# Second mixer to its feed-forward: squares from PSUM, x renewed in pairs of tiles, squares of x in the mixer, summed by TensorE in two halves

## What is computed

```
u_glu, q, k, v, gate_logits = split((rms_norm(x, pre_norm1) * (1 + sc1) + sh1) @ w_in)
...
y = (g_conv * y_conv + g_att * y_att) @ w_o
x = x + g1 * rms_norm(y, post_norm1)
h = rms_norm(x, pre_norm2) * (1 + sc2) + sh2
f = square(relu(h @ w_ff1)) @ w_ff2
x = x + g2 * rms_norm(f, post_norm2)
```

## Time and profile before

| | us |
|---|---|
| median of 3 runs (2768.16 to 2770.42) | 2768.65 |
| the profiled execution, its own time | 2776.59 |
| the profiled execution, span in the trace | 2774.8 |
| TensorE busy | 2628.9 (95%) |
| VectorE busy | 1464.5 (53%) |
| ScalarE busy | 926.0 (33%) |
| GpSimd busy | 1120.2 (40%) |
| granted TensorE clock, mean | 0.965 |

### The profile page before, as it was taken

The page is one execution under the profiler, slowest core; times in us unless marked ns, Lnnn a source line. Parts: engine busy times, 40 slices in busy tenths (PEclk is TensorE's granted clock), DMA queues, the critical chain, the costliest instruction groups (busy, mean ns, idle before and its releaser), DMA issues. The chain is left out here.

```text
span 2774.8 us, 32389 instructions
## 1 busy us (share of the span) xinstructions
PE 2628.9 (95%) x12740; PEld 2086.6 (75%) x12740; DVE 1464.5 (53%) x1794; ACT 926.0 (33%) x1314; POOL 1120.2 (40%) x505
## 2 busy tenths in 40 slices
PE   6999999999999999999999999599999999699997
PEld 4777778788888777778788887487776677488886
DVE  7884434843334885435753333498635563533333
ACT  4332443322223433343322221343234533222222
POOL 3333334344443433334344443178922223244442
PEclk9999999999999999999999999799989989799998
DMA  5222222343334222222343342232211112122331
GB/s 158 69 69 81 73 79 92 115 143 121 121 106 146 79 67 80 69 77 91 99 147 126 126 129 79 89 91 78 89 54 46 46 38 91 54 91 92 98 98 53
DMA packets 226619, 253.40 MB, mean 91 GB/s; under 512 B 9024, under 2 KB 202944, under 8 KB 226240
## 3 DMA queue, kind: packets, MB, share of 16 engines
q1 hardware_dynamic: 226176, 251.18, 28.8%
q10 hardware_dynamic: 320, 0.52, 0.1%
HBM read 246.96 MB, written 4.19 MB: 91 GB/s over the span
## 5 line engine op out<-in xcount | busy, mean ns | idle before, releaser
L217 POOL TENSOR_TENSOR sb_w_lo<-sb_raw,sb_w_hi 128x1024 fp32r<-128x1024 f32 x404 | 983.6, 2446 | 1416.7 <-ACT sb_w_hi L212 1414.9
L239 PE MATMUL ps<-sb_a_hi,sb_w_hi 128*128 128x512 f32 x1472 | 607.9, 413 | 35.6 <-POOL sb_w_lo L217 18.2
L212 ACT ACTIVATE sb_w_hi<-sb_raw 128x1024 fp32r<-128x1024 f32 x404 | 422.7, 1056 | 616.5 <-PE ps L241 537.8
L240 PE MATMUL ps<-sb_a_lo,sb_w_hi 128*128 128x512 f32 x1472 | 590.5, 401 | 0.0
L241 PE MATMUL ps<-sb_a_hi,sb_w_lo 128*128 128x512 f32 x1472 | 589.9, 401 | 0.0
L239 PE MATMUL ps<-sb_b_hi,sb_w_hi 128*128 128x512 f32 x960 | 381.3, 397 | 7.9 <-PEq L189 4.3
L239 PEld LDWEIGHTS ps<-sb_a_hi,sb_w_hi 128*128 128x128 f32 x1472 | 282.3, 192 | 134.6 <-issue 31.1
L240 PE MATMUL ps<-sb_b_lo,sb_w_hi 128*128 128x512 f32 x960 | 380.2, 396 | 0.0
L241 PE MATMUL ps<-sb_b_hi,sb_w_lo 128*128 128x512 f32 x960 | 380.0, 396 | 0.0
L241 PEld LDWEIGHTS ps<-sb_a_hi,sb_w_lo 128*128 128x128 f32 x1472 | 281.6, 191 | 69.5
L240 PEld LDWEIGHTS ps<-sb_a_lo,sb_w_hi 128*128 128x128 f32 x1472 | 282.6, 192 | 65.6 <-issue 2.4
(11 more groups left out here) (342 smaller groups left out, 2878.3 us busy)
## 6 DMA issues: line engine op xcount, KB each, us to landing
sb_raw<-in_w_in_dram SPq DMA_DIRECT2D x148, 512.0 KB, 3.7
sb_raw<-in_w_ffn_in_dram SPq DMA_DIRECT2D x88, 512.0 KB, 4.9
sb_raw<-in_w_ff_dram SPq DMA_DIRECT2D x64, 512.0 KB, 3.8
sb_ada<-in_w_ada_dram SPq DMA_DIRECT2D x48, 512.0 KB, 4.5
sb_raw<-in_w_ffn_out_dram SPq DMA_DIRECT2D x44, 512.0 KB, 3.8
sb_raw<-in_w_mix_o_dram SPq DMA_DIRECT2D x16, 512.0 KB, 3.4
sb_raw<-in_w_conv_o_dram SPq DMA_DIRECT2D x8, 512.0 KB, 3.4
sb_raw<-in_w_attn_o_dram SPq DMA_DIRECT2D x8, 512.0 KB, 3.3
```

The lines of the kernel that those rows point to most:

```text
L212: act.activation(w_hi[:, s, :], raw[:, s, :], ACT.Copy).then_inc(hi_done[s], 1)
L217: pool.tensor_tensor(w_lo[:, s, :], raw[:, s, :], w_hi[:, s, :].bitcast(F32), ALU.subtract)\
L239: pe.matmul(out, wh, hi, start=first and i == 0, stop=False)
L240: pe.matmul(out, wh, lo, start=False, stop=False)
```

## The change

In the mixer's "wo" groups ScalarE squares both tiles straight from PSUM, and then scales them by `gain_post` into `att` as it copies them; the banks come free after that. VectorE adds tiles 1 to 6 only, and TensorE sums tiles 0 and 7 with `n_sq=2`. VectorE and GpSimd renew x in pairs of tiles, in the form of the end of `ffn2`. ScalarE squares the renewed x into `c_pair_32` while still in the mixer, in the order of pairs 1, 0, 3, 2. The gains of `ffn2` are formed in the mixer, into columns 32 to 48 of `mod`, and the load of `par` in `ffn2` is gone. In `ffn2` TensorE begins with the sums over tiles 0 to 3 and over tiles 4 to 7, 16 matmuls each, and VectorE puts the two together with two small operations; ScalarE's squares and VectorE's adds are gone there. The counts of the semaphores shift accordingly.

```diff
@@ -142,6 +142,7 @@
         mod = mod_t[:, :]
+        ffn_gains = mod_t[:, 32:48]
         ps = top.enter_context(nc.psum_tensor("ps", [P, 8, T], F32))
@@ -1692,14 +1693,11 @@
                 act_in = sb(st, "f2_act_in", [P, 2, T])
-                par = sb(st, "f2_par", [P, NP2_COLS])
-                scale = sb(st, "f2_scale", [P, 16])
+                scale = ffn_gains
...
                     def _(sp):
-                        sp.dma_start(par[:, :], d["par2"][:, 0:NP2_COLS]).then_inc(small_in, 16)
-
@@ -1758,7 +1756,13 @@
                     def _(pe):
-                        pe_norm(pe, sq)
+                        pe_sum(pe, sq[:, 0:4, :], SUM_BANK, n_sq=4)
+                        for n in range(NB):
+                            for kt in range(4, KD):
+                                ins = pe.matmul(ps[:, SUM_BANK, NB + n:NB + n + 1], sq[:, kt, n * P:(n + 1) * P], ones[:, 0:1],
+                                                start=kt == 4, stop=kt == KD - 1)
+                        ins.then_inc(sums_done, 1)
+                        pe_spread(pe, rstd, SPREAD_BANK, rstd_done, 0)
                         h = [(h_hi[:, i, :], h_lo[:, i, :]) for i in range(KD)]
@@ -1813,14 +1817,13 @@
                         down(last_u + ups + 3, 0, last % 2, bank=0, start=False, tile_done=down_tile)
-                        pe.wait_ge(square_sum, 2)
-                        pe.wait_ge(squares, 2 * KD)
+                        pe.wait_ge(square_sum, 1)
+                        pe.wait_ge(squares, KD)
                         pe_sum(pe, sq[:, 0:KD:KD - 1, :], SUM_BANK, n_sq=2)
...
                     def _(act):
-                        act_squares(act, x, sq)
                         for n in range(rounded, SLOTS):
@@ -1868,16 +1871,13 @@
                         tt, ts, stt = dve.tensor_tensor, dve.tensor_scalar, dve.scalar_tensor_tensor
-                        dve.wait_ge(small_in, 16)
                         gain = scale[:, 0:8]
-                        step.done(stt(gain, mod[:, 32:40], 1.0, par[:, P2["pre_norm2"][0]:P2["pre_norm2"][1]],
-                                      ALU.add, ALU.mult))
-                        step.done(tt(scale[:, 8:16], mod[:, 40:48], par[:, P2["post_norm2"][0]:P2["post_norm2"][1]],
-                                     ALU.mult))
                         cm = Count(dve, mean_done)
                         nd = Count(dve, normed)
-                        dve_add_squares(dve, step, sq)
-                        dve_mean(dve, SUM_BANK, 0, cm)
+                        dve.wait_ge(sums_done, 2)
+                        half = rstd[:, NB:2 * NB]
+                        step.done(ts(half, ps[:, SUM_BANK, 0:NB], 1.0 / D, EPS, ALU.mult, ALU.add))
+                        cm.done(stt(rstd[:, 0:NB], ps[:, SUM_BANK, NB:2 * NB], 1.0 / D, half, ALU.mult, ALU.add))
                         dve.wait_ge(spread, 1)
@@ -1919,8 +1919,8 @@
                         def add_square(kt):
-                            dve.wait_ge(squares, KD + kt + 1)
-                            (Count(dve, square_sum, 1) if kt == KD - 2 else step).done(
+                            dve.wait_ge(squares, kt + 1)
+                            (Count(dve, square_sum) if kt == KD - 2 else step).done(
                                 tt(sq[:, 0, :], sq[:, 0, :], sq[:, kt, :], ALU.add))
@@ -1934,7 +1934,7 @@
                                 add_square(kt - 1)
-                        dve_mean(dve, SUM_BANK, 1, cm)
+                        dve_mean(dve, SUM_BANK, 2, cm)
                         dve.wait_ge(spread, 2)
@@ -2120,9 +2120,11 @@
                         pool_rsqrt(pool, 3)
-                        for kt in range(1, KD, 2):
-                            pool.wait_ge(x_done, 3 * (kt // 2) + 3)
-                            pool.tensor_tensor(x[:, kt, :], x[:, kt, :], q[:, kt, :], ALU.add).then_inc(x_done_odd, 1)
+                        pool.wait_ge(x_back, 16)
+                        for p in range(0, 4, 2):
+                            pool.wait_ge(pair_scaled, p // 2 + 1)
+                            two = slice(2 * p, 2 * p + 2)
+                            pool.tensor_tensor(x[:, two, :], x[:, two, :], q[:, two, :], ALU.add).then_inc(x_done_odd, 1)
@@ -2240,7 +2242,8 @@
-                        pe_sum(pe, conv, SUM_BANK, square_sum, 2)
+                        pe.wait_ge(squares, 3 * KD + KD)
+                        pe_sum(pe, conv[:, 0:KD:KD - 1, :], SUM_BANK, square_sum, 2, n_sq=2)
                         pe_spread(pe, rstd, SPREAD_BANK, rstd_done, 3)
@@ -2366,10 +2369,16 @@
-                                act.activation(att[:, two, :], src, ACT.Copy).then_inc(done, 1)
-                                emptied(act, gi)
-                                for t in (2 * p, 2 * p + 1):
-                                    act.activation(conv[:, t, :], att[:, t, :], ACT.Square).then_inc(squares, 1)
+                                for o in range(2):
+                                    act.activation(conv[:, 2 * p + o, :], src[:, o, :], ACT.Square).then_inc(squares, 1)
+                                for o in range(2):
+                                    t = 2 * p + o
+                                    ins = act.activation(att[:, t, :], src[:, o, :], ACT.Identity, scale=gain_post[:, t:t + 1],
+                                                         bias=0.0)
+                                    if o:
+                                        ins.then_inc(done, 1)
+                                    else:
+                                        step.done(ins)
                             if 17 <= gi <= 20:
@@ -2388,6 +2397,14 @@
+
+                        for p in (1, 0, 3, 2):
+                            if p % 2:
+                                act.wait_ge(x_done, p // 2 + 1)
+                            else:
+                                act.wait_ge(x_done_odd, p // 2 + 1)
+                            for t in (2 * p, 2 * p + 1):
+                                act.activation(c_pair_32[:, t, :], x[:, t, :], ACT.Square).then_inc(squares, 1)
@@ -2416,6 +2433,8 @@
                         step.done(tt(gain_post, mod[:, 16:24], pcol("post_norm1", 0, 8), ALU.mult))
+                        step.done(stt(ffn_gains[:, 0:8], mod[:, 32:40], 1.0, pcol("pre_norm2", 0, 8), ALU.add, ALU.mult))
+                        step.done(tt(ffn_gains[:, 8:16], mod[:, 40:48], pcol("post_norm2", 0, 8), ALU.mult))
                         step.done(ts(head_gain, pcol("head_norm"), 1.0 - LAM_INIT, None, ALU.mult))
@@ -2569,16 +2588,24 @@
                                 prod_rest(HEADS2 - 1, gc[:, HEADS2 - 1, :])
-                        dve_add_squares(dve, step, conv, 3 * KD, 1)
+                        for kt in range(1, KD - 1):
+                            dve.wait_ge(squares, 3 * KD + kt + 1)
+                            (Count(dve, square_sum, 1) if kt == KD - 2 else step).done(
+                                tt(conv[:, 0, :], conv[:, 0, :], conv[:, kt, :], ALU.add))
+                        dve.wait_ge(squares, 3 * KD + KD)
                         dve_mean(dve, SUM_BANK, 4, cm)
...
                         dve.wait_ge(x_back, 16)
-                        xd = Count(dve, x_done)
-                        for kt in range(KD):
-                            xd.done(stt(x[:, kt, :], x[:, kt, :], gain_post[:, kt:kt + 1], ps[:, SPREAD_BANK, :],
-                                        ALU.mult, ALU.mult))
-                            if kt % 2 == 0:
-                                xd.done(tt(x[:, kt, :], x[:, kt, :], q[:, kt, :], ALU.add))
+                        emptied(dve, len(G2) - 2)
+                        emptied(dve, len(G2) - 1)
+                        scaled_pair, xd = Count(dve, pair_scaled), Count(dve, x_done)
+                        row = ps[:, SPREAD_BANK, :].unsqueeze(1).to_broadcast([P, 2, T])
+                        for p in range(0, 4, 2):
+                            first, other = slice(2 * p, 2 * p + 2), slice(2 * p + 2, 2 * p + 4)
+                            scaled_pair.done(tt(x[:, first, :], x[:, first, :], row, ALU.mult))
+                            there = ps[:, p:p + 2, :]
+                            step.done(tt(there, x[:, other, :], row, ALU.mult))
+                            xd.done(tt(x[:, other, :], there, q[:, other, :], ALU.add))
                 phase_end()
```

## The result

The changed kernel is slower. Against the kernel before on the same chip the ratio is 1.0019, 95% interval 1.0011 to 1.0028 (medians 2775.88 and 2768.70 us, ten executions each). Two repeats gave 1.0018 (1.0009 to 1.0027) and 1.0015 (1.0006 to 1.0023). The means are 2775.6 us for the changed kernel (33 executions, standard error 0.4) and 2770.7 us for before (145 executions, 0.2, from five later sessions with means of their own between 2770.1 and 2771.2): 4.9 us. The ten executions of before in the first session, with a mean of 2769.5 (0.8), aren't among the 145; with them it would be 2770.6. Single executions of either kernel scatter by some 2.5 us, and with the clock: of 33 executions of before in one session, the fastest (2766.6) has a mean granted clock of 0.970, the slowest (2776.2) 0.966.

What follows compares the result with a forecast made beforehand. Bound: TensorE, 95% busy, and a slackless chain between mixer and feed-forward. The mixer gives 2.85 us, the sum takes back 4.0 and 0.2: net 1.4 us slower, 2768.65 to 2770.05 us; range 2767.3 to 2773.7 (8 in 10).

Steps and rivals of the forecast that it cites:

- The stretch: From ScalarE's release by the mixer's last matmul to the feed-forward's first big matmul: 36.1 us before, 1.4 us longer forecast.
- Part 1: Mixer's end, squares straight from PSUM: TensorE's two-tile sum starts 1.8 us earlier, takes 1.9 us, ends at 2359.65.
- Part 2: Mixer's end, x renewed in pairs of tiles: 7.5 us instead of 11.6.
- Part 3: Squares of x in the mixer: ScalarE ends at 2373.0, barrier 1.2 us, feed-forward opens at 2374.2 instead of 2377.05.
- Part 4: Feed-forward's opening: TensorE's sum in two halves, 64 passes at the low clock, 13.2 us; before, opening to sum's end 9.19.
- rival A: Feed-forward's opening: clock rises inside the 64-pass sum, 9.0 us instead of 13.2; 2764.2 us in all; chance 0.07.
- the clock's term: First big matmuls behind the sum: time at the low clock, at most 1.1 us either way, taken as nothing.
- B: Feed-forward's first big matmuls: clock stays low, half a microsecond per microsecond; 2774.8 us at 15 us low; chance 0.04.
- C: Mixer's end doesn't save its 2.85 us; stage opens at 2377.05, loss 4.2 us, 2772.9 us; chance 0.07.

Runs made afterwards that it cites:

- the run with the clock kept up: The changed kernel with 34 unused big matmuls on TensorE between the mixer's spread and its barrier; mean 2776.0 us.
- the third run: The changed kernel, but VectorE adds all eight tiles of squares at the feed-forward's opening and TensorE sums one; mean 2768.4 us, ratio to before 0.9987.

## Why the prediction was wrong

The measured time lies 5.8 us above the forecast, outside the range, and nearly none of that comes from the chain that I had worked out. The stretch was sized well: 1.4 us longer was forecast, 1.6 measured (37.78, mean of three, against 36.15, mean of the five with before's form). By its steps:

- *Part 1*: two-tile sum 1.54 us after the release and 1.92 us long (forecast 1.47 and 1.9), renewal 6.89 us after it (6.97). Right.
- *Part 2*: 7.51 us, as in the earlier trace rows. Right; squares on ScalarE beside it slow nothing.
- *Part 3*: ScalarE's end 16.63 us behind the release (16.7), the barrier 1.05 us (1.2). The stage opened 17.7 us behind the release, 17.9 forecast. Right, but the move on its own was worth nothing, as the run below tells.
- *Part 4*: 13.8 us instead of 13.2. The term was mis-sized by 0.6: passes followed each other by 0.213 us (32 in 6.82), above my 0.20. I had read it from the count of 34 in 6.80 us, but that count takes in passes already under way at the window's start: in the same trace of before, 32 passes start from 1998.67 to 2005.29, 0.213 apart. The low clock from the first pass to the last was right, and rival A fell: TensorE was busy without a gap for 13.8 us and the granted clock read 0.50 throughout. By the rule of the Trainium skill, page "TensorE: Matmul & The Clock Gate", section "Part 1: The HAM clock gate", that sustained matmul activity releases the throttle, it should have risen; these sums are matmuls, and in the three traces of after neither sum raised it. The measurement decides.

The step that failed is the last one, from the stretch to the time. I wrote that whatever gets longer on the chain moves the end by as much, took the median of three executions as the kernel's time, costed the gains at nothing, and took nothing for the clock, with 1.1 us at most either way, at one place behind the stretch. Of the 5.8 us between 2770.1 and 2775.9:

- 2.0 us is the base: three executions with a median of 2768.65, of a kernel whose mean over 145 is 2770.7, and whose executions scatter by 2.5 us. With it the forecast is 2772.1, inside its own range.
- 0.2 us is the stretch.
- 2.8 us goes with a lower clock over the whole kernel. The mean granted clock is on record for each of these executions, to 0.001: it averages 0.9663 (0.0002) over the 33 of after and 0.9677 (0.0001) over the 145 of before. A line fitted through the 145 of before gives 2.0 us for each 0.001. The difference of 0.0014 is then 2.8 us, which is an estimate, and 2.05 us (0.23) are left between the kernels at the same clock, near to the 1.6 of the stretch. The mean times by clock, with the number of executions, say the same without a fit:

| mean granted clock | before, us | after, us |
|---|---|---|
| 0.965 | 2778.1 (1) | 2778.0 (9) |
| 0.966 | 2774.4 (22) | 2776.5 (11) |
| 0.967 | 2771.9 (28) | 2773.9 (6) |
| 0.968 | 2770.1 (65) | 2772.4 (7) |
| 0.969 and 0.970 | 2767.8 (29) | none |

- The rest, 0.8 us, is 0.3 between mean and median, and for the other 0.5 within the errors.

So the clock's term was mis-sized: nothing, with 1.1 us at one place, where it comes to some 2.8 us over the kernel. That is read off a relation between executions, and no run changed the clock alone; the mean also counts time in which TensorE does nothing useful (the run with the clock kept up has 0.9675 at the time of after). Why after runs at the lower clock more often stays open. It isn't the step between the stages: the clock is low around it for 37.6 us in the first trace of before (2360.3 to 2397.9) and for 37.5 in that of after (2357.2 to 2394.7). The gains, which I had costed at nothing by VectorE's idle time of 14.84 us, have a part in it. With them put back 2.8 us come back, and the mean clock is 0.9671 (0.0003); by the same line that is 1.6 us of the 2.8. With two unused operations it is 0.9673 (0.0002), 0.9 us of their 2.1. The idle time is there, and what makes 2 us of it wasn't found.

One place where part of this can be seen is the tail, which the change doesn't touch. It takes 19.8 us in the traces of after and 18.8 in those with before's form (means of three and of five), because in all three of after the clock falls some half microsecond into the last sum, which then takes 3.1 us instead of 1.92 to 2.78. But that isn't set by the length of the stretch: with the gains back, at stretches of 38.01 and 37.91, the tails are 18.6 and 19.9, and with the adds in the mixer, at 28.11 and 28.19, they are 20.0 and 18.5.

Rivals B and C didn't happen: the first big matmuls came up at about 2394.7, 4.9 us after the first (before: 5.5), and the mixer saved its 3 us. **Was part 3 worth its place?** 

> Parts 1 and 2 alone (squares from PSUM, two tiles summed, x in pairs; the gains stay in the mixer): the squares of x, the seven adds and the sum of 8 passes stand in the feed-forward as before. By the rows: 36.4 us of before (mean of two traces), less 1.05 for the sum, 4.1 for the renewal and 1.1 because the adds no longer wait for the gains: a stretch of 30.1 us, 6.3 below before. Theory 1: that stretch, no worse than with the squares in the mixer (30.9), since there four squares stand bare before the barrier and here all but 1.1 us of them lies beside the adds. Rival (moving the squares into the mixer is worth something): 2 us or more above the third run.

```diff
-# mixer, ScalarE: the eight squares of the renewed x
+# feed-forward, ScalarE: act_squares(act, x, sq); VectorE: dve_add_squares; TensorE: one tile
```

Its stretch is 30.14 us, as forecast (30.1), against 30.88 with the squares in the mixer; mean 2767.7 (0.8), ratio 0.9986 (0.9977 to 0.9994); a worth of 2 us or more for the move isn't there. ScalarE's squares in the feed-forward lie beside the adds and show for 1.2 us; in the mixer four of them stand bare for 2.2 us. So parts 1 and 2, with the gains out of the way of the adds (1.2 us in the run that moved them alone), are the whole gain of this change, 6.0 us of stretch, and part 4 gives back more than that, 6.9. Part 3 pays only together with the adds in the mixer: 28.11.

The fastest version has parts 1, 2 and 3, the adds in the mixer in pairs and the gains at its end: mean 2765.0, against 2770.7 before and 2775.6 after. That is 0.2% below before, and some 8 us of shorter stretch show as 5.7 us.

## What to carry to other kernels

A sum over partitions by one-column matmuls costs TensorE 0.213 us for each fp32 pass at the low clock, and 64 of them behind an idle time ran at it from the first to the last: let VectorE add in its idle time, in pairs of tiles (1.22 us for two), and leave TensorE eight passes. Before forecasting one or two tenths of a per cent, take the base from tens of executions, and look how far single traces of the same kernel lie apart: here 7 us in one stage. Compare executions at the same granted clock: it separates what the change does on its chain (2.0 us here) from what goes with the clock (2.8 us). And measure the small companions of a change alone: here two operations of 0.2 us each, in an idle time, came with 2 us, of which the clock accounts for less than half.

## What the runs showed of the hardware

- The barrier between stages takes 1.05 us behind ScalarE (2368.68 to 2369.73), 1.13 behind GpSimd and 1.29 behind VectorE (2374.92 to 2376.21 in the run with the adds in the mixer).
- Sums of one-column matmuls let the clock fall though TensorE is busy without a gap, and none raised it from 0.50 in 13.8 us. In the one trace where it was kept up, it held for 3.3 us after the last big matmul (2370.06 to 2373.4).
- Over 145 executions of before, the time falls by 2.0 us for each 0.001 of mean granted clock (correlation -0.87). After has 9 of 33 executions at 0.965, before 1 of 145.
- Two unused operations in VectorE's idle time, with a longer buffer, came with a mean 2.1 us (0.7) higher, and eight with 1.0 (0.8).
